# Two transformer blocks on one core: 96 tokens instead of 64 taken out of the dense expert products

## The chip, the cores and the metric

One Trainium2 chip, one core of it. The time is device microseconds of one launch. Single-core program, so there is one span and one granted TensorE clock.

## What is computed

512 tokens of width 1024 go through two blocks. The first ends in a layer of 16384 tiny experts, of which every token uses 128 (8 heads times 16); the second is attention with a gated feed-forward part and is not touched here. Cut to the expert layer:

```python
def block(xb):                                   # 128 tokens at a time
    q = (xb @ w_q).reshape(p, 8, 2, 64)
    sc = einsum('phcd,hcnd->phcn', q, sub_keys)  # 2 x 128 scores per head
    top_s, top_i = lax.top_k(sc, 16)
    cand_s = top_s[:, :, 0, :, None] + top_s[:, :, 1, None, :]
    best_s, best_pos = lax.top_k(cand_s, 16)     # 16 experts per head
    idx = take_along_axis(cand_i, best_pos)      # number = first * 128 + second
    g = softmax(best_s)
    act = gelu(einsum('phkd,pd->phk', expert_u[idx], xb))
    return einsum('phk,phkd->pd', g * act, expert_v[idx])
```

All in float32; the kernel splits each float32 operand into a high and a low float32r part and makes three products of them.

## The kernel before

**Dense and picked tokens.** The experts are 16 groups (`N_GROUPS`) of 8 tiles (`GROUP`) of 128. For the first `DT = T - PICKED` tokens (448) the kernel computes all 16384 experts densely: 128 U products `hidden = gelu(U h)`, a multiplication by a sparse table of coefficients (`weight`, "mix"), and 128 V products. Each product is one weight block of 128x1024 and 24 matmuls of 128x128 against `DT` columns (`partial`: 16 with the high weights, then 8 with the low ones). The last `PICKED` tokens (64) go another way: their 128 experts each are fetched as rows by number and used by VectorE alone. 64 tokens fill 128 partitions twice, so token t stands on two partitions with half of its experts each, and one indirect DMA fetches one row of 1024 per partition (512 KB).

**Row steps** (`row_step(q)` on VectorE, `load_rows(q)` on GpSimd). Steps 0 to `PICKED - 1` multiply a row of U by the token and sum (`row_coef`); then one gelu on ScalarE; steps `PICKED` to `2 * PICKED - 1` add coefficient times row of V to `own_sum`. The rows go round `ROWS` = 4 buffers; a load waits for the step that used its buffer before. At the end one matmul per output tile with `fold` adds the two partitions of each token. `ROW_STEPS` spreads the 128 steps evenly over the V slots of groups i = 1 to 14.

**Order of stages.** `w_in`, `w_out`, `w_q`; then the U stage: 120 U products (`AHEAD` = 15 groups), whose hidden tiles of 14 groups (`KEPT`) are put into DRAM. Beside it VectorE routes (`route_tokens`, four blocks of 128 tokens): for blocks 0 and 1 GpSimd scatters the 256 sets of coefficients into DRAM by accumulating indirect DMAs; for blocks 2 and 3 they are made by one-hot products, four tokens at a time ("quads": `make_hot`, four 256-wide matmuls at `place`, `placed_quad`). `QUADS_AT` says at which U product a quad is made: block 2 has 32 quads, block 3 has (448 - 384) / 4 = 16, one at every second product from number 83.
Then the loop over `MIX_ORDER` = 14, 15, 0, 1, ..., 13, whose index is i. At i = 0 the last 8 U products run, each beside one mix step of group 14; then each group has 8 V slots (k = 0 to 7). A slot has on VectorE: `split_lo` of the weight block of the next slot (`lo = raw - hi`), one `mix_tile` of the next group with its low part (`finish_mix`), at i = 0 an addition to the residual that waits for the slot's V product, then the row steps of that slot. ScalarE makes the high parts of the weights and of the mix. 17 steps of a rotation table (`table_steps`) stand one per slot in later groups.

**Queues.** SyncE loads weight blocks into `RAW` = 3 buffers, each when the low part three blocks before is made. GpSimd's in-order queue has, per group, its row loads, and after the fourth of them `load_group(i + 2)`: coefficient table and hidden tiles, 1792 KB each (128 x 8 x 448 x 4 bytes), which go through the same DMA queue as the rows. It waits first for the scatter to end and for the last stores of stage.

Of the kernel before, what the change touches and what calls it, by code (L numbers as in the profile page):

```python
# [37 lines left out]
PICKED = 64  # L38
DT = T - PICKED
ROWS = 4  # L40
SCATTERED = 2
ROUTE_STEPS = HEADS + HEADS // 2 + 4 + 2
# [141 lines left out]
def build(nc, a, out_cols, values, counting):  # L184

    with ExitStack() as ctx:
# [6 lines left out]
        def signal(name, step=1):  # L193
# [19 lines left out]
        scattered = [signal(f"scattered{tb}", 16) for tb in range(SCATTERED)]  # L213
        rows_landed = [signal(f"rows{i}_landed", 16) for i in range(ROWS)]
# [88 lines left out]
        own_x = sb("own_x", [P, D], F32, scope)  # L303
# [3 lines left out]
        fold = sb("fold", [P, PICKED], F32, scope)  # L307
        route = ExitStack()
        top_s = sb("top_s", [P, HEADS, 2, TOPK], F32, route)
# [30 lines left out]
        mixed = [(mixed_hi, mixed_lo), (h_hi, h_lo), (last_hi, last_lo)]  # L340
        position = sb("position", [P, T], I32, scope)
        turns = sb("turns", [P, T], F32, scope)
        own_sum = sb("own_sum", [P, D], F32, scope)
        rows = [sb(f"rows{i}", [P, D], F32, scope)[:] for i in range(2)] \
            + [t[:].rearrange("p k t -> p (k t)") for t in (square, scaled)]
# [124 lines left out]

        ROW_STEPS = {}
        for q in range(2 * PICKED):
            ROW_STEPS.setdefault(divmod(GROUP + q * (N_GROUPS - 2) * GROUP // (2 * PICKED), GROUP), []).append(q)

# [64 lines left out]
        def tensor():  # L539
# [280 lines left out]
            for i, g in enumerate(MIX_ORDER):  # L820
# [4 lines left out]
                for k in range(KD):  # L825
# [3 lines left out]
                    else:  # L829
# [277 lines left out]
        def scalar():  # L1107
# [523 lines left out]
        def vector():  # L1631
# [304 lines left out]
            def route_tokens(tb):  # L1936
# [84 lines left out]
            V.tensor_tensor(fold[:], const("ident")[:, 0:PICKED], const("ident")[:, PICKED:P], ALU.add).then_inc(*dve.inc("fold"))  # L2021
# [4 lines left out]
            ada_columns(40, 48, 0.0, "gate2")  # L2026
            for j in range(AHEAD * GROUP):
# [54 lines left out]
            def row_step(q):  # L2082

                kind, s = divmod(q, PICKED)
                row = rows[q % ROWS]
                if q == 0:
                    V.wait_ge(*act["own_x", 1])
# [4 lines left out]
                if kind == 0:  # L2092
                    V.tensor_tensor_reduce(out=row, in0=row, in1=own_x[:], scale=1.0, scalar=0.0, op0=ALU.mult, op1=ALU.add,  # L2093
                                           accum_out=row_coef[:, s:s + 1]).then_inc(*dve.inc(("row", q)))
                elif s == 0:
                    V.tensor_scalar(own_sum[:], row, row_coef[:, 0:1], None, ALU.mult).then_inc(*dve.inc(("row", q)))
# [750 lines left out]
```

## Time and profile before

| | |
|---|---|
| median of 3 runs | 2380.35 us (2378.09 to 2387.47) |
| profiled execution | 2381.73 us, span 2380.4 us |
| granted TensorE clock, mean | 0.987 |
| busy: PE, PEld | 2313.4, 2025.2 us |
| busy: DVE, ACT, POOL | 1578.9, 856.4, 951.0 us |
| U products 0 to 127 | 310 to 979 us |
| V products | 979 to 1603 us |

PE is TensorE's matmuls, PEld its weight loads, DVE VectorE, ACT ScalarE, POOL GpSimd, SP SyncE. A busy PE is not a PE at its peak; what tells its pace is the distance from the start of one matmul to the start of the next. "weights_lo" written by DVE is `split_lo`; "hidden<-hidden,weight" and "mixed_lo" or "h_lo" are the two parts of a mix step; "CUSTOM_DVE" on rows is a U row step; "own_sum<-rows,row_coef,own_sum" is a V row step. In a row, the bracket is the engine's idle time before the instruction and what ended it.

### The profile page before, as it was taken

The numbers are of one execution on the slowest core, as the hardware profiler recorded it, in microseconds if no ns is written. First come the engines' busy times: TensorE is split into PE (matmuls) and PEld (weight loads), VectorE is DVE, ScalarE is ACT, GpSimd is POOL, SyncE is SP. The second block draws the span as 40 slices with busy tenths as digits, with TensorE's granted clock in tenths as the row PEclk, the third lists the DMA queues.
The fourth block names the chain that finished last, engine by engine and source line by source line (L and its number), as shares of the span: only waits on it lengthen the run. The fifth ranks groups of instructions, "written<-read, shape, count | busy, mean of one in ns | idle before, by whom it ended". The sixth has DMA issues, their size and how long they took to land.

```text
span 2380.4 us, 29901 instructions
## 1 busy us (share of the span) xinstructions
PE 2313.4 (97%) x11272; PEld 2025.2 (85%) x11272; DVE 1578.9 (66%) x3014; ACT 856.4 (36%) x1335; POOL 951.0 (40%) x602
## 2 busy tenths in 40 slices
PE   6999999999899999999999999999999989999998
PEld 3777889999789999999999999998887778888887
DVE  6774699889996553588777777764856556434333
ACT  4433443333334333333333333353345534322221
POOL 1444208788888770033333433343332331111100
PEclk9999999999999999999999999999999999999999
DMA  7658746666667676579888888842424252333332
GB/s 289 195 148 251 211 138 170 162 153 160 163 150 188 169 182 206 196 301 343 322 321 330 315 349 298 300 132 86 130 67 116 70 188 89 97 97 98 102 98 76
DMA packets 199798, 443.60 MB, mean 186 GB/s; under 512 B 49180, under 2 KB 108700, under 8 KB 195104
## 3 DMA queue, kind: packets, MB, share of 16 engines
q1 hardware_dynamic: 139960, 319.12, 41.1%
q0 software_dynamic: 59696, 122.58, 17.3%
q8 instruction: 91, 1.49, 0.3%
q14 instruction: 51, 0.42, 0.1%
HBM read 374.06 MB, written 65.21 MB: 185 GB/s over the span
## 4 chain that ended last, share of the span: by engine, by line
PE 68%; DVE 3%; ACT 1%; issue 0%; ACTq 0%
PE bank L558 18%; PE bank L559 18%; PE bank L562 18%; PE bank_stat L935 1%; PE bank_stat L936 1%; PE bank_stat L940 1%; PE bank_stat L558 1%; PE bank_stat L562 1%; PE bank_stat L559 1%; DVE hot_weight L2010 1%; PE bank L967 1%; PE bank L965 1%; PE bank L980 1%; PE bank L710 1%; DVE weights_lo L1643 0%; PE bank_stat L585 0%
## 5 line engine op out<-in xcount | busy, mean ns | idle before, releaser
L558 PE MATMUL bank<-h_lo,weights_hi 128*128 128x448 f32 (+1 forms) x2148 | 813.8, 379 | 8.5 <-DVE gates L2311 3.8
L559 PE MATMUL bank<-h_hi,weights_hi 128*128 128x448 f32 (+1 forms) x2148 | 809.7, 377 | 0.0
L1119 ACT ACTIVATE weights_hi<-weights_raw 128x1024 fp32r<-128x1024 f32 (+1 forms) x411 | 432.1, 1052 | 498.1 <-PE bank L562 364.0
L1643 DVE TENSOR_TENSOR weights_lo<-weights_raw,weights_hi 128x1024 fp32r<-128x1024 f32 x351 | 443.6, 1264 | 196.9 <-ACT weights_hi L1119 194.5
L2489 POOL DMA_INDIRECT expert_coefs<-square x256 | 443.0, 1730 | 155.4 <-issue 79.0
L562 PE MATMUL bank<-h_hi,weights_lo 128*128 128x448 f32 (+1 forms) x2148 | 499.5, 374 | 1.4 <-DVE weights_lo L1643 1.4
L558 PEld LDWEIGHTS bank<-h_lo,weights_hi 128*128 128x128 f32 x2148 | 408.9, 190 | 61.3 <-DVE gates L2311 3.9
L559 PEld LDWEIGHTS bank<-h_hi,weights_hi 128*128 128x128 f32 x2148 | 408.5, 190 | 49.9 <-issue 0.2
L562 PEld LDWEIGHTS bank<-h_hi,weights_lo 128*128 128x128 f32 x2148 | 403.0, 188 | 52.3 <-DVE weights_lo L1643 2.5
L2436 POOL TENSOR_TENSOR weights_lo<-weights_raw,weights_hi 128x1024 fp32r<-128x1024 f32 x60 | 147.6, 2465 | 223.5 <-ACT weights_hi L1119 223.4
L1330 ACT ACTIVATE hidden<-bank 128x448 f32<-128x448 f32 x128 | 69.9, 546 | 406.4 <-PE bank L562 406.4
L558 PE MATMUL bank<-mixed_lo,weights_hi 128*128 128x448 f32 x456 | 166.5, 365 | 0.0
L559 PE MATMUL bank<-mixed_hi,weights_hi 128*128 128x448 f32 x456 | 166.5, 365 | 0.0
L2559 POOL TENSOR_TENSOR silu<-silu,ffn_scale 128x512 f32<-128x512 f32 x22 | 33.7, 1532 | 208.0 <-ACT silu L1614 208.0
L562 PE MATMUL bank<-mixed_hi,weights_lo 128*128 128x448 f32 x456 | 101.7, 365 | 0.0
L558 PEld LDWEIGHTS bank<-mixed_lo,weights_hi 128*128 128x128 f32 x456 | 85.7, 188 | 6.8
L562 PEld LDWEIGHTS bank<-mixed_hi,weights_lo 128*128 128x128 f32 x456 | 85.7, 188 | 6.8
L559 PEld LDWEIGHTS bank<-mixed_hi,weights_hi 128*128 128x128 f32 x456 | 85.6, 188 | 6.7
L2447 POOL TENSOR_TENSOR scaled<-scaled,square 128x512 f32<-128x512 f32 x18 | 25.5, 1416 | 150.5 <-ACT square L1266 148.9
L2061 DVE TENSOR_TENSOR hidden<-hidden,weight 128x448 f32<-128x448 f32 x128 | 79.1, 618 | 0.0
L2517 POOL DMA_INDIRECT rows<-in_rows_u,row_at x32 | 45.7, 1430 | 76.6 <-DVE row_coef L2093 73.9
L2548 POOL TENSOR_SCALAR scaled<-scaled,att_stats 128x384 f32<-128x384 f32 (+1 forms) x32 | 44.6, 1407 | 78.7 <-DVE att_stats L2288 78.7
(463 smaller groups left out, 3424.7 us busy)
## 6 DMA issues: line engine op xcount, KB each, us to landing
weights_raw<-in_expert_u SPq DMA_DIRECT2D x128, 512.0 KB, 3.8
weights_raw<-in_expert_v SPq DMA_DIRECT2D x128, 512.0 KB, 4.6
weight<-expert_coefs POOLq DMA_DIRECT2D x16, 1792.0 KB, 10.0
hidden_store<-hidden SPq DMA_DIRECT2D x28, 896.0 KB, 6.1
hidden<-hidden_store POOLq DMA_DIRECT2D x14, 1792.0 KB, 15.1
ada_raw<-in_w_ada SPq DMA_DIRECT2D x34, 512.0 KB, 6.1
expert_coefs<-zeros SPq DMA_DIRECT2D x32, 512.0 KB, 6.4
expert_coefs<-stage SPq DMA_DIRECT2D x12, 1024.0 KB, 5.8
```

The costliest lines, as they stand in the source:

```text
L558: M.matmul(bank[:, 0:width], hi[:, c:c + P], m_lo[k][:, 0:width], start=start and i == 0, stop=False)
L559: M.matmul(bank[:, 0:width], hi[:, c:c + P], m_hi[k][:, 0:width], start=False, stop=False)
L562: ins = M.matmul(bank[:, 0:width], lo[:, c:c + P], m_hi[k][:, 0:width], start=False, stop=stop and i == len(tiles) - 1)
L1119: S.activation(w_hi[n % SPLIT][:, 0:w], w_raw[n % RAW][:, 0:w], ACT.Copy).then_inc(*hi_done.inc(n))
L1330: S.activation(hidden[g % 2][:, n, :], banks["u", j][:, 0:DT], ACT.Gelu).then_inc(*act.inc(("u", j)))
L1643: V.tensor_tensor(w_lo[n % SPLIT][:, 0:w], w_raw[n % RAW][:, 0:w], w_hi[n % SPLIT][:, 0:w].bitcast(F32), ALU.subtract).then_inc(*lo_dve.in ...
L2061: V.tensor_tensor(v, v, weight[g % 2][:, :, n, :], ALU.mult).then_inc(*dve.inc(("mixed", g, n)))
L2436: G.tensor_tensor(w_lo[n % SPLIT][:, 0:w], w_raw[n % RAW][:, 0:w], w_hi[n % SPLIT][:, 0:w].bitcast(F32), ALU.subtract).then_inc(*lo_pool.i ...
L2489: G.indirect_dma_start(out=coef_store[:], out_offset=bass.IndirectOffsetOnAxis(ap=place_at[:, tb, c:c + 1], axis=0), in_=share[:, tb, c:c ...
L2517: G.indirect_dma_start(out=rows[q % ROWS], out_offset=None, in_=a[("rows_u", "rows_v")[kind]], in_offset=bass.IndirectOffsetOnAxis(ap=row_ ...
L2548: G.tensor_scalar(p, p, stats[:, u, 2:3], None, ALU.mult).then_inc(*pool.inc(("att_prob", u)))
L2559: G.tensor_tensor(silu[:, f % 2, :], silu[:, f % 2, :], ffn_scale[:], ALU.mult).then_inc(*pool.inc(("silu", f)))
```

## The change

`PICKED` becomes 96 and `DT` 416. The 96 tokens are taken in three batches of 32; in a batch each token stands on four partitions with a quarter of its experts. There are 192 row steps instead of 128, over 124 slots: the second four U slots of i = 0 and all V slots of i = 0 to 14 (before: 112 slots). `ROWS` is 5, the fifth buffer lying where the table's source and scratch lie, so its first load waits for the end of `table_steps`; those now run three per U slot at i = 0. The tokens are copied once onto their partitions by 12 DMAs (`copy_own`, on SyncE's queue after the last quad) in place of four ScalarE copies. `fold` adds four identity columns in three chained steps, and stands behind the first eight routing steps; the closing product is three 32-wide matmuls per tile instead of one of 64. Block 3 has (416 - 384) / 4 = 8 quads. The routing numbers of the picked tokens are made by two operations and 24 copies of 32x32 instead of six operations. `load_group` comes after the fifth row load of a group.

```diff
-PICKED = 64
+PICKED = 96
+BATCH = 32
+BATCHES = PICKED // BATCH
 DT = T - PICKED
-ROWS = 4
+ROWS = 5
...
+        SLOTS = [(0, "u", n) for n in range(HALF, GROUP)] + [(i, k) for i in range(N_GROUPS - 1) for k in range(KD)]
         ROW_STEPS = {}
         for q in range(2 * PICKED):
-            ROW_STEPS.setdefault(divmod(GROUP + q * (N_GROUPS - 2) * GROUP // (2 * PICKED), GROUP), []).append(q)
+            ROW_STEPS.setdefault(SLOTS[q * len(SLOTS) // (2 * PICKED)], []).append(q)
...
-            room = min(QUADS, AHEAD * GROUP - 2 - first)
+            room = min(n_quads * TB // 2, QUADS, AHEAD * GROUP - 2 - first)
...
-                            ins = M.matmul(held_bank(k)[:, DT:T], own_sum[:, k * P:(k + 1) * P], fold[:], start=True, stop=True)
+                            for b in range(BATCHES):
+                                ins = M.matmul(held_bank(k)[:, DT + b * BATCH:DT + (b + 1) * BATCH], own[b][:, k * P:(k + 1) * P],
+                                               fold[:], start=True, stop=True)
...
-                    for half in range(2):
-                        S.activation(own_x[half * PICKED:(half + 1) * PICKED, c * T:(c + 1) * T], banks["own_x", c][0:PICKED, :], ACT.Copy) \
-                            .then_inc(*act.inc(("own_x", c) if half else ("own_x_first", c)))
+                    S.activation(own_tokens_x[0:PICKED, c * T:(c + 1) * T], banks["own_x", c][0:PICKED, :], ACT.Copy) \
+                        .then_inc(*act.inc(("own_x", c)))
...
-                    for half, to in enumerate((slice(64, 128), slice(0, 64))):
-                        slots = slice(half * PICKED, (half + 1) * PICKED)
-                        V.tensor_copy(row_share[to, :], chosen[64:128, 2, slots]).then_inc(*dve.inc(("row_share", half)))
-                        chain(V.scalar_tensor_tensor(row_coef[to, :], chosen[64:128, 0, slots], float(N_KEYS), chosen[64:128, 1, slots],
-                                                     ALU.mult, ALU.add))
-                        chain(V.tensor_copy(row_at[to, :], row_coef[to, :]), ("row_at", half))
+                    chain(V.scalar_tensor_tensor(place_f, chosen[:, 0, :], float(N_KEYS), chosen[:, 1, :], ALU.mult, ALU.add))
+                    chain(V.tensor_copy(column_u, place_f), "row_numbers")
+                    for b in range(BATCHES):
+                        tokens = slice(P - PICKED + b * BATCH, P - PICKED + (b + 1) * BATCH)
+                        columns_of = slice(b * BATCH, (b + 1) * BATCH)
+                        for part in range(P // BATCH):
+                            to = slice(part * BATCH, (part + 1) * BATCH)
+                            V.tensor_copy(row_share[to, columns_of], chosen[tokens, 2, to]).then_inc(*dve.inc(("row_share", b, part)))
+                            V.tensor_copy(row_at[to, columns_of], column_u[tokens, to]).then_inc(*dve.inc(("row_at", b, part)))
...
                 if q == 0:
-                    V.wait_ge(*act["own_x", 1])
+                    V.wait_ge(*own_copied[BATCHES - 1, P // BATCH - 1])
...
                         split_lo(BLOCK_AT["expert_u", (g + 1) * GROUP + n] + 2)
+                        for _ in range(TABLE_STEPS // GROUP + 1):
+                            next(turning, None)
+                        for q in ROW_STEPS.get((i, "u", n), ()):
+                            row_step(q)
...
             load_group(0)
+            G.dma_start(position[:], a["positions"]).then_inc(*position_landed.inc("position"))
             load_group(1)
-            G.dma_start(position[:], a["positions"]).then_inc(*position_landed.inc("position"))
...
                 if q >= ROWS:
                     G.wait_ge(*dve["row", q - ROWS])
+                elif rows[q] is rows[-1]:
+                    G.wait_ge(*dve["angle"])
...
-            for half in range(2):
-                G.wait_ge(*dve["row_at", half])
-            load_group(2)
-            for i in range(1, len(MIX_ORDER)):
+            G.wait_ge(*dve["row_at", BATCHES - 1, P // BATCH - 1])
+            G.wait_ge(*own_copied[BATCHES - 1, P // BATCH - 1])
+            for n in range(GROUP):
+                for q in ROW_STEPS.get((0, "u", n), ()):
+                    load_rows(q)
+            for i in range(len(MIX_ORDER)):
...
+            def copy_own():
+
+                Y.wait_ge(*dve["routed", TB - 1])
+                Y.wait_ge(*act["own_x", 1])
+                for b in range(BATCHES):
+                    for part in range(P // BATCH):
+                        Y.dma_start(own[b][part * BATCH:(part + 1) * BATCH, :], own_tokens_x[b * BATCH:(b + 1) * BATCH, :]) \
+                            .then_inc(*own_copied.inc((b, part)))
```

## Rows read from the trace of the kernel before

**Rows 1.** The page: busy time, and VectorE's share in 40 slices.

```profile
PE 2313.4 (97%) x11272; PEld 2025.2 (85%) x11272; DVE 1578.9 (66%) x3014; ACT 856.4 (36%) x1335; POOL 951.0 (40%) x602
DVE  6774699889996553588777777764856556434333
```

**Rows 2.** Timeline (start, duration, engine, line): first matmul of two V blocks.

```profile
1105.43 0.36 PE L558 MATMUL bank<-h_lo,weights_hi 128*128 128x448 f32 x1
...
1144.34 0.36 PE L558 MATMUL bank<-mixed_lo,weights_hi 128*128 128x448 f32 x1
```

**Rows 3.** Timeline of PE: matmuls with 512 columns, then with 256.

```profile
2200.60 0.39 PE L558 MATMUL bank<-h_lo,weights_hi 128*128 128x512 f32 x1
...
2206.04 0.39 PE L558 MATMUL bank<-h_lo,weights_hi 128*128 128x512 f32 x1
...
2362.19 0.28 PE L710 MATMUL bank<-ffn_lo,weights_hi 128*128 128x256 f32 x1
...
2363.99 0.28 PE L710 MATMUL bank<-ffn_hi,weights_hi 128*128 128x256 f32 x1
```

**Rows 4.** Timeline of PE: two U blocks with a quad's products between.

```profile
750.80 1.78 PE L562 MATMUL bank<-h_hi,weights_lo 128*128 128x448 f32 x8
752.42 0.64 PE L805 MATMUL bank<-hot_weight,one_hot 128*128 128x256 f32 x4
756.14 1.78 PE L562 MATMUL bank<-h_hi,weights_lo 128*128 128x448 f32 x8
```

**Rows 5.** Windows: length, busy of PE, PEld, DVE, ACT, POOL, clock, DMA share, GB/s.

```profile
354.00:536.00 182.00, 182.00 (x902) 168.67 (x900) 158.75 (x508) 62.98 (x84) 145.53 (x86) 1.00 0.67 164
548.00:732.00 184.00, 168.31 (x842) 152.30 (x842) 182.09 (x543) 65.56 (x123) 156.86 (x90) 0.97 0.68 163
742.00:905.00 163.00, 163.00 (x832) 151.55 (x831) 92.89 (x209) 56.59 (x96) 121.74 (x71) 1.00 0.72 175
940.00:1570.00 630.00, 630.00 (x3112) 583.95 (x3111) 457.02 (x604) 206.01 (x272) 203.40 (x156) 1.00 0.79 296
```

**Rows 6.** Timeline of DVE in a V group: a row stall, then one slot.

```profile
1186.82 1.22 DVE L2093 CUSTOM_DVE_ANT_0 rows<-rows,own_x 128x1024 f32<-128x1024 f32 x1
...
1192.30 1.23 DVE L2093 CUSTOM_DVE_ANT_0 rows<-rows,own_x 128x1024 f32<-128x1024 f32 x1 [4.25 <-DMA rows<-in_rows_u,row_at]
...
1193.44 1.22 DVE L1643 TENSOR_TENSOR weights_lo<-weights_raw,weights_hi 128x1024 fp32r<-128x1024 f32 x1
...
1195.65 1.22 DVE L2093 CUSTOM_DVE_ANT_0 square<-square,own_x 128x1024 f32<-128x1024 f32 x1
...
1196.80 1.22 DVE L1643 TENSOR_TENSOR weights_lo<-weights_raw,weights_hi 128x1024 fp32r<-128x1024 f32 x1
```

**Rows 7.** The same view, later: two row steps of V in one slot.

```profile
1357.94 2.66 DVE L2099 SCALAR_TENSOR_TENSOR own_sum<-rows,row_coef,own_sum 128x1024 f32<-128x1024 f32 x2
```

**Rows 8.** Timeline of POOL: the group's hidden tiles, then the next row load.

```profile
1174.75 0.60 POOL L2506 DMA_DIRECT2D hidden<-hidden_store  x1
1175.66 1.41 POOL L2517 DMA_INDIRECT rows<-in_rows_u,row_at  x1 [0.30 <-issue]
```

**Rows 9.** Windows, columns as in rows 5: inside that burst, and a whole group.

```profile
1185.00:1190.00 5.00, 5.00 (x27) 4.63 (x26) 3.04 (x5) 1.56 (x3) 0.94 (x1) 1.00 0.99 415
...
1183.00:1222.00 39.00, 39.00 (x195) 36.14 (x194) 28.21 (x43) 12.34 (x16) 13.07 (x11) 1.00 0.85 323
```

**Rows 10.** Timeline of POOL: the last scatter, then the first tables.

```profile
895.13 1.54 POOL L2489 DMA_INDIRECT expert_coefs<-square  x1 [0.30 <-issue]
913.66 1.18 POOL L2502 DMA_DIRECT2D weight<-expert_coefs  x2 [16.99 <-DMA expert_coefs<-stage]
```

**Rows 11.** Timeline of DVE at i = 0: the residual waits for its product.

```profile
1013.21 0.68 DVE L2114 SCALAR_TENSOR_TENSOR residual<-bank,ada,residual 128x448 f32<-128x448 f32 x1 [1.98 <-PE bank L562]
```

**Rows 12.** Timeline of PE in the last group: two closing products.

```profile
1577.68 0.33 PE L837 MATMUL bank<-fold,own_sum 128*128 128x64 f32 x2
...
1582.77 0.33 PE L837 MATMUL bank<-fold,own_sum 128*128 128x64 f32 x2
```

More of the change, by code:

```diff
@@ L37 @@
 QUADS = P // 4
-PICKED = 64
+PICKED = 96
+BATCH = 32
+BATCHES = PICKED // BATCH
 DT = T - PICKED
-ROWS = 4
+ROWS = 5
 SCATTERED = 2
+TABLE_STEPS = 17
 ROUTE_STEPS = HEADS + HEADS // 2 + 4 + 2
@@ L213, in build @@
         scattered = [signal(f"scattered{tb}", 16) for tb in range(SCATTERED)]
+        own_copied = signal("own_copied", 16)
         rows_landed = [signal(f"rows{i}_landed", 16) for i in range(ROWS)]
@@ L302, in build @@
         hidden.append(sb("hidden1", [P, GROUP, DT], F32, scope))
-        own_x = sb("own_x", [P, D], F32, scope)
         row_at = sb("row_at", [P, PICKED], U32, scope)
@@ L306, in build @@
         row_coef = sb("row_coef", [P, PICKED], F32, scope)
-        fold = sb("fold", [P, PICKED], F32, scope)
+        fold = sb("fold", [P, BATCH], F32, scope)
+        sb("row_spacer", [P, 64], F32, scope)
         route = ExitStack()
+        sb("route_spacer", [P, 1408], F32, route)
         top_s = sb("top_s", [P, HEADS, 2, TOPK], F32, route)
@@ L340, in build @@
         mixed = [(mixed_hi, mixed_lo), (h_hi, h_lo), (last_hi, last_lo)]
+        over = ExitStack()
+        row_over = sb("row_over", [P, D], F32, over)
+        over.close()
         position = sb("position", [P, T], I32, scope)
         turns = sb("turns", [P, T], F32, scope)
-        own_sum = sb("own_sum", [P, D], F32, scope)
+        own = [sb(f"own{b}", [P, D], F32, scope) for b in range(BATCHES)]
         rows = [sb(f"rows{i}", [P, D], F32, scope)[:] for i in range(2)] \
-            + [t[:].rearrange("p k t -> p (k t)") for t in (square, scaled)]
+            + [t[:].rearrange("p k t -> p (k t)") for t in (square, scaled)] + [row_over[:]]
+        own_tokens_x = scaled[:].rearrange("p k t -> p (k t)")
         scope.close()
@@ L2019, in placed_quad @@
                     V.tensor_tensor(at, placed_part(tb, quad, half, 1), at, ALU.add).then_inc(*dve.inc(("place", tb, quad, half)))
-            V.tensor_tensor(fold[:], const("ident")[:, 0:PICKED], const("ident")[:, PICKED:P], ALU.add).then_inc(*dve.inc("fold"))
             routers = [route_tokens(tb) for tb in range(TB)]
@@ L2026, in vector @@
             ada_columns(40, 48, 0.0, "gate2")
+            chain(V.tensor_tensor(fold[:], const("ident")[:, 0:BATCH], const("ident")[:, BATCH:2 * BATCH], ALU.add))
+            chain(V.tensor_tensor(fold[:], fold[:], const("ident")[:, 2 * BATCH:3 * BATCH], ALU.add))
+            chain(V.tensor_tensor(fold[:], fold[:], const("ident")[:, 3 * BATCH:P], ALU.add), "fold")
             for j in range(AHEAD * GROUP):
@@ L2082, in row_step @@
             def row_step(q):
-                kind, s = divmod(q, PICKED)
+                kind, c = divmod(q, PICKED)
+                b, s = divmod(c, BATCH)
                 row = rows[q % ROWS]
                 if q == 0:
-                    V.wait_ge(*act["own_x", 1])
+                    V.wait_ge(*own_copied[BATCHES - 1, P // BATCH - 1])
                 if q == PICKED:
@@ L2092, in row_step @@
                 if kind == 0:
-                    V.tensor_tensor_reduce(out=row, in0=row, in1=own_x[:], scale=1.0, scalar=0.0, op0=ALU.mult, op1=ALU.add,
-                                           accum_out=row_coef[:, s:s + 1]).then_inc(*dve.inc(("row", q)))
+                    V.tensor_tensor_reduce(out=row, in0=row, in1=own[b][:], scale=1.0, scalar=0.0, op0=ALU.mult, op1=ALU.add,
+                                           accum_out=row_coef[:, c:c + 1]).then_inc(*dve.inc(("row", q)))
                 elif s == 0:
-                    V.tensor_scalar(own_sum[:], row, row_coef[:, 0:1], None, ALU.mult).then_inc(*dve.inc(("row", q)))
+                    V.tensor_scalar(own[b][:], row, row_coef[:, c:c + 1], None, ALU.mult).then_inc(*dve.inc(("row", q)))
                 else:
                     V.wait_ge(*dve["row", q - 1])
-                    V.scalar_tensor_tensor(own_sum[:], row, row_coef[:, s:s + 1], own_sum[:], ALU.mult, ALU.add) \
+                    V.scalar_tensor_tensor(own[b][:], row, row_coef[:, c:c + 1], own[b][:], ALU.mult, ALU.add) \
                         .then_inc(*dve.inc(("row", q)))
@@ L2120, in vector @@
                         dve.also(("held", k), ("x2", g, k))
-                    if i >= len(MIX_ORDER) - KEPT:
-                        next(turning, None)
                     for q in ROW_STEPS.get((i, k), ()):
@@ L2658, in sync @@
                     store_stage(*LAST_QUAD)
+                    copy_own()
                 load_weights(BLOCK_AT["expert_u", j] + 5)
```

4 lines of the change are left out of this document (2 added, 2 removed).

## The prediction

> **What bounds the kernel now.** I read the page first: PE is busy 97% and VectorE 66%, but VectorE's slices run from 3 to 9 tenths [rows 1], so the mean hides stages with different limits. Then the timeline of PE for its pace. In the V groups the first matmuls of two blocks eight apart are 38.91 us apart: 4.864 us per block of 24 matmuls, or 202.7 ns each [rows 2], and PE never stops from 940 to 1570 us [rows 5]. So there the pace of PE is the time. The windows over the U stage show three parts [rows 5]: U products 8 to 47 (354 to 536 us, PE full, VectorE 158.8 of 182 us), the 32 quads of block 2 (548 to 732 us, VectorE 182.1 of 184 us, PE only 168.3), and from 742 us on PE full again with VectorE little used. Only in the second is VectorE the bound; the first eight U products are another such place (VectorE at 9 tenths there [rows 1], my reading).
>
> **A dense block gets 32 columns shorter.** 448 columns take 202.7 ns [rows 2], 512 take (2206.04 - 2200.60) / 24 = 226.7 ns, 256 take 1.80 / 15 = 120 ns [rows 3]. From 256 to 512 that is 0.417 ns per column, so 32 columns are 13.3 ns and a block 24 x 13.3 = 0.32 us. 416 columns are not in the trace: 448 costs 2.7 ns more than the line of the other two widths (200.0). The line gives 186.7 ns for 416, the slope from 448 to 512 gives 190.7. I take 189.3, which keeps 448's excess, so 4.544 us per block; both ends stay in the range. The weight loads lie 120 ns apart where matmuls have 256 columns [rows 3], so they set no floor at 189.
> Beside it a rule. The Trainium skill (TensorE: Matmul & The Clock Gate, Back-to-back issue gap) gives sustained spacings of 81 ns for 128 columns and 131 ns for 512, 0.13 ns per column; by it a block would lose 24 x 4.2 = 0.10 us only. The trace's spacings are other ones, and its slope is three times that.
>
> **Where these 0.32 us count.** There are 256 such blocks. The first 8 are paced by VectorE, and so are the 32 of block 2's quads, whose VectorE work the change leaves alone: the stretch stays 184 us whatever PE could do [rows 5]. Elsewhere 256 - 40 = 216 blocks x 0.32 = **69.1 us**, if VectorE keeps up. For U products 8 to 47: 158.8 us of work in 182 x 4.544 / 4.864 = 170 us; it fits. From 742 us it fits easily, and block 3 makes 8 quads fewer. A block with a quad takes 756.14 - 750.80 = 5.34 us against 4.86 [rows 4], so 8 x 0.48 = **3.8 us** more.
>
> **Small things.** The closing product costs 5.09 - 4.86 = 0.22 us per tile [rows 12]; three of half the width I bound between twice and three times that plus nothing for the width, +0.14 to +0.45 us, and take 0.28: 8 tiles, **-2.2 us**. `fold` becomes three chained small operations in VectorE's first stretch: 0.3 us (0 to 0.6, an estimate: two operations more, far smaller than the 0.54 us that one of 448 columns takes [rows 6]). The 24 small copies come after product 80, where VectorE is idle half the time [rows 5], so nothing; without that cover some 3 us. `copy_own` puts 12 issues and 1.5 MB in front of a weight load on SyncE. In that stretch DMA is 72% busy [rows 5]; the transfer is 1.5 MB at 415 GB/s [rows 9], 3.7 us. Weight blocks are three ahead, so I take 1 us of 0 to 5. The four ScalarE copies that go save nothing, ScalarE is 36% busy [rows 1]. Sum so far: 69.1 + 3.8 - 2.2 - 0.3 - 1.0 = 69.4 us.
>
> **Scatter and tables.** GpSimd's scatter has its own pace and ends at 895 us; the first tables then waited 17 us for the last stores of `stage` [rows 10]. Those stores come 16 products earlier now. The U stage is some 30 us shorter (80 x 0.32 + 3.8), so the first mix of group 14, at about 937 us before, wants its table at 907; issued at about 900 us it lands by 911. VectorE waits some 4 us there; with 93 of 163 us busy in the stretch before [rows 5] it comes there far ahead of PE, so PE sees nothing. What is late next here is the scatter itself.
>
> **The V groups: is VectorE still covered?** One slot with one row step takes 1196.80 - 1193.44 = 3.36 us of VectorE: a low part 1.13, two mix parts 0.54 each, the row step 1.15 [rows 6]. Mixes get 0.03 us shorter each. A V row step costs about 1.19 alone, 1.28 when it follows another (2.66 for two, overlap taken in) [rows 7]. After the change a group has 192 x 8 / 124 = 12.4 row steps instead of 9.1: 8 x 2.13 + 12.4 x 1.15 = 31.3 us in the U half, 32.2 us in the V half. PE takes 8 x 4.544 = 36.35 us. So 5.0 and 4.1 us per group are left, where there were 38.9 - 28 = 11.
> Against this stands the stall behind the group's burst. GpSimd issues hidden tiles at 1174.75 and a row load right behind at 1175.66 [rows 8]; VectorE waits 4.25 us for that row until 1192.30 [rows 6], so the row needs 16.6 us. In the burst DMA is full at 415 GB/s [rows 9]. After the change the burst is 0.26 MB smaller (0.6 us), and four rows lie ready instead of three: 4 / 1.55 slots x 4.544 = 11.7 us of cover where there were 12.5. Stall: 16.6 - 0.6 - 11.7 = 4.3, or 6 us if VectorE runs at its own pace and eats the rows sooner. I take 4.6, near the stall seen. The group then needs 35.9 us in the U half (covered by 36.35) and 36.8 to 38.4 in the V half (not covered). The first group, i = 0, is the tightest: its residual additions hold VectorE to PE's pace with 2 us idle per slot [rows 11], and 1.5 row steps now go there, so VectorE enters group 1 with no lead. I cost it at 1.2 us there, 0.5 us in each of 7 groups of the U half and 0.7 us in each of 7 of the V half, rounded to **-10 us**; 0 to 20 by the ends of the stall.
> Is DMA itself full? Per group 8 weight blocks 4.2 MB, rows 6.5 MB, tables and hidden tiles 3.4 MB: 14.1 MB, 34.0 us at 415 GB/s, against 36.35. Before it was 12.65 MB in 38.9 us, 325 GB/s, which the window confirms (323, share 0.85) [rows 9]. So DMA goes from 85% to about 95% of what it can do. That is the thinnest cover of all.
>
> **Sum.** 69.4 - 10 = 59.4 us off the profiled execution of 2381.7: 2322.3. The median of the runs stands 1.4 us below that execution, so **2321 us**, 2.5% less.
>
> **Rivals.**
> (A) All cover holds and 416 columns fall on the line: nothing lost in the V groups (2311), and 216 x 24 x 2.7 ns = 14 us more from the width (2297). For it: a full lead of VectorE before the change. 22%.
> (B) Rows become the pace of the V groups. With a stall of 6.2 to 9 us a group takes 37.5 to 40.3 us in the U half and 38.4 to 41.2 in the V half; over 7 and 8 groups 25 to 66 us of the 69 are given back: 2335 to 2377, middle 2345. For it: DMA near full, one in-order queue for rows and tables. Against it: the burst gets smaller and the buffers more. 20%.
> (C) DMA from HBM is capped below what the burst shows. If a whole group could sustain only 358 GB/s, 14.1 MB take 39.4 us, 15 x 3.05 = 46 us lost: 2357. For it: no whole group has shown over 330. Against it: 415 GB/s over 5 us, more than once [rows 9]. 4%. The Trainium skill (DMA: Bandwidth & Descriptors, its table at the head) gives 358 GB/s as the limit of HBM per core. The trace exceeds it in the burst.
> (D) Slower than before. The same stall at 11 us: if each of 12.4 row loads per group waits for its full turn behind tables and weights, a group takes 42.3 and 43.2 us, 96 us lost, 27 more than all gains: about 2407. It decides at a group of 36.35 + 69.4 / 15 = 41.0 us, a stall of about 9. Seen so far: 4.25 in the rows above. 5%.
> (E) The change doesn't do what it says: the distance between matmuls stays near 203 ns at 416 columns. Then the gain is 3.8 us of quads less 3.5 of small things: 2380. 4%. By the skill's spacings above, 216 x 0.10 = 22 us would be gained.
> Forecast (2311 to 2335, likeliest 2321): 45%.
>
> **How the numbers follow.** The range takes in A nearly to its end and B past its middle: 2298 to 2357; outside are the last of A, B beyond 2357, half of C, D and E, together some 19%. A measurement of this kernel tells about 0.5% (12 us) from no change. Faster by more than that, under 2368: forecast, A, C and nearly all of B, 0.89. Within: E and the end of B, 0.06. Slower: D, 0.05.
>
> **What would show it.** Right: V blocks 4.54 us apart nearly everywhere; the window of block 2's quads still 184 us with VectorE at 99%; U stage ending near 900 us; one row stall of 4 to 6 us per group, DMA share near 0.95. Wrong: PE waiting for weights_lo in most groups (B), DMA full through whole groups (C), matmuls 203 ns apart (E), or PE waiting for mixed at i = 0, which would make the scatter the late one.

## The result and the profile after

The changed kernel takes 2364.91 us (median of 5 runs, 2362.95 to 2367.24), the kernel before 2380.35 (5 runs, 2378.09 to 2387.47): ratio 0.9931, interval 0.9914 to 0.9948. So 15 us were gained by the medians, 17 by the profiled executions, of the 59 predicted, and the time lies above the upper end of the range. The profiled execution is 2364.91 us, its span 2363.6.

Where the time went is read from four marks: the gelu of U product 0, the gelu of U product 120, the last closing product, the end of the span. The column "predicted" is the prediction's sum split over the same stretches.

| stretch, us | before | predicted | after |
|---|---|---|---|
| to U product 0 | 310.0 | 310.3 | 311.0 |
| U product 0 to 120 | 635.1 | 606.7 | 603.4 |
| U product 120 to last closing product | 658.1 | 626.8 | 673.2 |
| from there to the end | 777.2 | 777.2 | 776.0 |
| span | 2380.4 | 2321.0 | 2363.6 |

The U stage came out as forecast, 3 us better. The V stage got 15 us longer where it was to get 31 us shorter. All of the miss is there: 46.4 us, of which the other stretches give 3.8 back.

The page of after, its busy times and the chain that ended last (answers to [rows 1]):

```profile
PE 2249.3 (95%) x11272; PEld 2031.7 (86%) x11272; DVE 1616.6 (68%) x3044; ACT 850.0 (36%) x1317; POOL 1062.2 (45%) x666
...
PE 34%; DMA 11%; DVE 11%; POOL 3%; issue 2%; ACT 1%; DVEq 0%; ACTq 0%
```

PE was 68% of that chain before and VectorE 3%; now DMA and VectorE have 11% each, most of it in lines named after rows. PE's busy time fell by 64 us, the span by 17: the rest is idle time of PE. The pace of PE where nothing holds it, from the timeline of PE (start, duration, engine, line), two pairs of U blocks and then a pair of closing products, the answer to [rows 2, 12]:

```profile
503.48 0.35 PE L568 MATMUL bank<-h_lo,weights_hi 128*128 128x416 f32 x1
...
506.50 1.67 PE L572 MATMUL bank<-h_hi,weights_lo 128*128 128x416 f32 x8
508.00 0.35 PE L568 MATMUL bank<-h_lo,weights_hi 128*128 128x416 f32 x1
...
862.21 1.66 PE L572 MATMUL bank<-h_hi,weights_lo 128*128 128x416 f32 x8
...
866.69 1.66 PE L572 MATMUL bank<-h_hi,weights_lo 128*128 128x416 f32 x8
...
1571.51 0.75 PE L848 MATMUL bank<-fold,own 128*128 128x32 f32 x6
...
1576.72 0.75 PE L848 MATMUL bank<-fold,own 128*128 128x32 f32 x6
```

A block takes 508.00 - 503.48 = 4.52 us early in the U stage and 866.69 - 862.21 = 4.48 us later (there from one block's low products to the next one's): 188.3 and 186.7 ns per matmul of 416 columns. The closing product lies 5.21 us apart, 0.69 to 0.73 more than a block without it.

The windows (length, busy of PE, PEld, DVE, ACT, POOL, clock, DMA share, GB/s) over U products 8 to 47, over block 2's quads, over the rest of the U stage, and over the whole V stage, the answers to [rows 5]:

```profile
354.00:536.00 182.00, 182.00 (x971) 180.89 (x970) 171.68 (x553) 67.43 (x92) 140.78 (x83) 1.00 0.70 171
545.00:730.00 185.00, 164.05 (x851) 158.17 (x850) 180.66 (x543) 65.12 (x123) 157.56 (x91) 0.94 0.67 161
742.00:905.00 163.00, 163.00 (x884) 162.57 (x883) 66.32 (x115) 56.03 (x86) 129.41 (x78) 1.00 0.74 182
926.00:1588.00 662.00, 624.59 (x3221) 607.90 (x3220) 531.29 (x704) 220.92 (x288) 330.18 (x228) 0.97 0.88 329
```

In the last one PE stands 37 us, and it starts matmuls below its pace beside that: the granted clock is 0.97 there, where it was 1.00 [rows 5]. Before the change PE was full from 940 to 1570.

**One V group, as they all go.** POOL's timeline, the group's burst and the row loads around it (answer to [rows 8]); then VectorE's (answer to [rows 6]); then PE's:

```profile
1156.25 0.58 POOL L2521 DMA_DIRECT2D weight<-expert_coefs  x1
1156.80 0.61 POOL L2525 DMA_DIRECT2D hidden<-hidden_store  x1
1157.71 1.38 POOL L2538 DMA_INDIRECT row_over<-in_rows_u,row_at  x1 [0.30 <-issue]
...
1176.68 1.68 POOL L2538 DMA_INDIRECT row_over<-in_rows_u,row_at  x1 [7.90 <-DVE row_coef L2110]
```

```profile
1166.36 1.22 DVE L2110 CUSTOM_DVE_ANT_0 scaled<-scaled,own 128x1024 f32<-128x1024 f32 x1
1167.50 0.08 DVE L2110 DVE_READ_ACCUMULATOR2_ANT row_coef<- 128x1 f32 x1
1175.18 1.23 DVE L2110 CUSTOM_DVE_ANT_0 row_over<-row_over,own 128x1024 f32<-128x1024 f32 x1 [7.60 <-DMA row_over<-in_rows_u,row_at]
1176.33 0.08 DVE L2110 DVE_READ_ACCUMULATOR2_ANT row_coef<- 128x1 f32 x1
1176.33 1.22 DVE L1654 TENSOR_TENSOR weights_lo<-weights_raw,weights_hi 128x1024 fp32r<-128x1024 f32 x1
```

```profile
1177.60 3.14 PE L572 MATMUL bank<-h_hi,weights_lo 128*128 128x416 f32 x8 [2.94 <-DVE weights_lo L1654]
1180.55 0.55 PE L568 MATMUL bank<-h_lo,weights_hi 128*128 128x416 f32 x1
```

The row asked for at 1157.71, right behind 3.4 MB of tables and hidden tiles, is used at 1175.18: it is 17.5 us on its way (the "way"). The rows that lie ready last VectorE until 1167.58, 9.9 us (the "cover"). The difference, 7.6 us, VectorE stands; the low part of the next weight block is queued behind the row step, starts at 1176.33, and PE, which has gone on meanwhile, starts its low products only at 1177.60, when that part is done.

The stop has a second price on PE. These eight products take 2.95 us to the next start where the eight at 506.50 above take 1.50: the window around them shows a mean granted clock of 0.75, so part of it passed at the lower of the two levels (1.2 GHz in place of 2.4).

```profile
1175.00:1180.00 5.00, 2.40 (x7) 2.30 (x8) 4.82 (x8) 1.50 (x2) 1.71 (x2) 0.75 1.01 389
```

By the mean of 0.97 some 40 us of the V stage passed at that level (an estimate: 0.03 x 2 x 662). It does not set the time of a group: VectorE, at whose pace the groups go, waits in them for nothing that PE makes.

This happens once per group, 14 times from 977 us on: the row is 17.2 to 19.4 us on its way (mean 17.8), the ready rows cover 9.9 to 12.3 us (mean 10.5), the stall is 6.1 to 9.1 us (mean 7.3). VectorE's waits for rows in the V stage, by tile:

```profile
DVE row_over L2110 <- DMA row_over<-in_rows_u,row_at: 28.4, 4, 7.6
DVE own L2116 <- DMA scaled<-in_rows_v,row_at: 26.5, 4, 6.9
DVE rows L2110 <- DMA rows<-in_rows_u,row_at: 22.6, 3, 8.2
DVE own L2116 <- DMA rows<-in_rows_v,row_at: 17.5, 3, 9.1
DVE own L2113 <- DMA rows<-in_rows_v,row_at: 7.4, 1, 7.4
DVE square L2110 <- DMA square<-in_rows_u,row_at: 6.5, 2, 6.1
```

With 0.2 us more that is 109.1 us; before, the same sum was 44.3. What VectorE waited for otherwise has gone: before, 44.8 us for `weights_hi` and 40.2 for `mixed_hi`, which ScalarE makes at PE's pace; after, none. So VectorE has no lead left to pay a stall from, and a group takes VectorE's own work plus the stall: from one stall's end to the next, 38.3 to 42.1 us, 39.85 on average (13 groups from 977.44 to 1495.47), where PE alone would need 36.

### The profile page after: what moved, and what is told of

Its sections match the earlier page's. It is cut to its first block, busy times and chain, and to the rows that moved or that the text cites. A ratio compares the mean times of both kernels' runs of the same rounds, so it can differ in the third digit from the quotient of the medians.

```text
span 2363.6 us, 29994 instructions
## 1 busy us (share of the span) xinstructions
PE 2249.3 (95%) x11272; PEld 2031.7 (86%) x11272; DVE 1616.6 (68%) x3044; ACT 850.0 (36%) x1317; POOL 1062.2 (45%) x666
## 4 chain that ended last, share of the span: by engine, by line
PE 34%; DMA 11%; DVE 11%; POOL 3%; issue 2%; ACT 1%; DVEq 0%; ACTq 0%
PE bank L568 8%; PE bank L572 8%; PE bank L569 8%; DMA row_over<-in_rows_u,row_at 2%; DMA rows<-in_rows_v,row_at 2%; DVE own L2116 2%; DMA scaled<-in_rows_v,row_at 2%; DVE weights_lo L1654 2%; DMA square<-in_rows_u,row_at 2%; DMA rows<-in_rows_u,row_at 2%; DVE hidden L2077 1%; PE bank_stat L947 1%; PE bank_stat L948 1%; PE bank_stat L952 1%; DVE rows L2110 1%
## 5 line engine op out<-in xcount | busy, mean ns | idle before, releaser
L568 PE MATMUL bank<-h_lo,weights_hi 128*128 128x416 f32 (+1 forms) x2148 | 796.0, 371 | 10.2 <-DVE gates L2330 3.8
L569 PE MATMUL bank<-h_hi,weights_hi 128*128 128x416 f32 (+1 forms) x2148 | 791.1, 368 | 0.0
L572 PE MATMUL bank<-h_hi,weights_lo 128*128 128x416 f32 (+1 forms) x2148 | 482.8, 366 | 15.8 <-DVE weights_lo L1654 15.4
L1342 ACT ACTIVATE hidden<-bank 128x416 f32<-128x416 f32 x128 | 66.2, 518 | 347.2 <-PE bank L572 331.6
L568 PE MATMUL bank<-mixed_lo,weights_hi 128*128 128x416 f32 x456 | 163.5, 358 | 6.6 <-ACT mixed_hi L1406 6.2
L569 PE MATMUL bank<-mixed_hi,weights_hi 128*128 128x416 f32 x456 | 161.6, 354 | 0.0
L572 PE MATMUL bank<-mixed_hi,weights_lo 128*128 128x416 f32 x456 | 102.2, 369 | 17.9 <-DVE weights_lo L1654 17.9
L2538 POOL DMA_INDIRECT rows<-in_rows_v,row_at x39 | 62.4, 1599 | 61.1 <-DVE own L2116 45.4
L2538 POOL DMA_INDIRECT rows<-in_rows_u,row_at x39 | 56.7, 1454 | 59.3 <-DVE row_coef L2110 53.5
L2077 DVE TENSOR_TENSOR hidden<-hidden,weight 128x416 f32<-128x416 f32 x128 | 74.7, 583 | 10.0 <-DMA weight<-expert_coefs 9.9
```

Of the source, the lines that this page charges most:

```text
L568: M.matmul(bank[:, 0:width], hi[:, c:c + P], m_lo[k][:, 0:width], start=start and i == 0, stop=False)
L569: M.matmul(bank[:, 0:width], hi[:, c:c + P], m_hi[k][:, 0:width], start=False, stop=False)
L572: ins = M.matmul(bank[:, 0:width], lo[:, c:c + P], m_hi[k][:, 0:width], start=False, stop=stop and i == len(tiles) - 1)
L1342: S.activation(hidden[g % 2][:, n, :], banks["u", j][:, 0:DT], ACT.Gelu).then_inc(*act.inc(("u", j)))
L2077: V.tensor_tensor(v, v, weight[g % 2][:, :, n, :], ALU.mult).then_inc(*dve.inc(("mixed", g, n)))
L2538: G.indirect_dma_start(out=rows[q % ROWS], out_offset=None, in_=a[("rows_u", "rows_v")[kind]], in_offset=bass.IndirectOffsetOnAxis(ap=row_ ...
```

## Experiments

Three theories could make the V stage long. **T1**: the row loads stand in one in-order queue behind the burst; neither VectorE nor DMA is full by itself. **T2**: VectorE has no room for 12.4 row steps per group. **T3**: DMA has no room for the bytes of a group. The kernels before in these runs had medians of 2380.86 to 2383.23, so ratios are given. "V stage" is the stretch from U product 120 to the last closing product, 673.2 us in the changed kernel.

**1. The burst in eight pieces (spread8).** Four over the token sets of the table, four over pairs of hidden tiles, one behind each row load from the second on.

```diff
-            def load_group(i):
+            def group_parts(i):
...
-                    G.dma_start(weight[g % 2][:].rearrange("p s j t -> p (s j t)"),
-                                coefs[g].rearrange("p s j t -> p (s j t)")).then_inc(*weight_landed[g % 2].inc(g))
+                    for c in range(4):
+                        s = slice(c * n_s // 4, (c + 1) * n_s // 4)
+                        G.dma_start(weight[g % 2][:, s].rearrange("p s j t -> p (s j t)"),
+                                    coefs[g][:, s].rearrange("p s j t -> p (s j t)")).then_inc(*weight_landed[g % 2].inc((g, c)))
...
+                        yield
...
-                    if n == ROWS - 1:
-                        load_group(i + 2)
+                    if n >= 1:
+                        next(parts, None)
```

> The changed kernel with each group's table and hidden tiles (3.4 MB) fetched in 8 pieces, one behind each of 8 row loads, instead of two transfers behind the fifth row load. Theory 1 (the row load queued behind that burst stalls VectorE some 7 us per group, and VectorE has only 4 to 5 us to spare): the stall falls under 2 us, V groups come to 36.2 to 36.6 us instead of 37.8 to 43.3, and the whole takes 2310 to 2325 us. Theory 2 (VectorE's row steps are simply too much work) and theory 3 (DMA is full over whole groups): within 5 us of the changed kernel, 2360 to 2370.

Measured: 2331.03 us (2328.03 to 2333.69), ratio 0.9777 (0.9761 to 0.9794), V stage 635.8. The same bytes, the same row steps, 34 us less than the changed kernel: only their order in the queue is another. VectorE's row waits fall from 109.1 to 66.6 us, in 58 small ones of at most 5.3. The time is 6 us above the range that T1 expected. POOL's timeline shows what it still pays:

```profile
994.00 0.57 POOL L2525 DMA_DIRECT2D weight<-expert_coefs  x1 [6.19 <-DVE h_lo L1696]
994.88 1.35 POOL L2554 DMA_INDIRECT rows<-in_rows_u,row_at  x1 [0.30 <-issue]
```

The first piece now comes so early that its buffer is still in use by the mix of the group before; POOL waits 6.19 us for that mix, with all row loads behind it.

**2. What is each resource worth alone?** no_rows leaves out the row loads and the row steps, loads_only the steps alone (each load waits for the landing of the one that used its buffer), steps_only all row loads but the first five (the steps then work on stale rows, and those of U with a factor of 0.02 in place of 1). All three leave out or falsify the part of the output that belongs to the 96 picked tokens.

```diff
 def row_step(q):
+                if q == PICKED - 1:
+                    V.memset(row_coef[:], 0.0).then_inc(*dve.inc(("row", q)))
...
+                return
```

```diff
 def load_rows(q):
                 if q >= ROWS:
-                    G.wait_ge(*dve["row", q - ROWS])
+                    return
```

> The changed kernel without row loads and without row steps (the picked tokens' expert part is left out). All theories: V groups at PE's pace, 36.2 us, about 2305 us; it gives the floor of the narrower products. If it stays above 2340, the loss is in none of the rows' parts.

> The changed kernel with all 192 row loads but without VectorE's row steps (left out); a load waits for the landing five before in place of the step. Theory 1 and 2: V groups at 36.2 us, about 2307 us, DMA share about 0.95. Theory 3: groups stay at 38 us or more, 2340 or more, with DMA share near 1.0 throughout.

> The changed kernel with all 192 row steps on VectorE but only the first five row loads (the others are left out; the steps work on what lies in the buffers). Theory 1 and 3: V groups at 36.2 to 36.5 us, about 2310 us, PE never waiting for weights_lo. Theory 2: groups stay at 38 us or more, 2345 or more.

| | us | ratio (interval) | V stage |
|---|---|---|---|
| no_rows | 2302.28 | 0.9661 (0.9641 to 0.9680) | 608.9 |
| loads_only | 2307.92 | 0.9684 (0.9665 to 0.9704) | 614.1 |
| steps_only | 2308.79 | 0.9688 (0.9663 to 0.9713) | 621.1 |
| changed kernel | 2364.91 | 0.9931 (0.9914 to 0.9948) | 673.2 |

The windows 1100 to 1500 of the changed kernel, loads_only and steps_only, in this order:

```profile
1100.00:1500.00 400.00, 377.07 (x1930) 366.58 (x1929) 321.27 (x413) 126.69 (x163) 208.68 (x145) 0.97 0.94 355
```

```profile
1100.00:1500.00 400.00, 400.00 (x2132) 397.59 (x2130) 195.98 (x263) 136.19 (x182) 147.21 (x146) 1.00 0.92 364
```

```profile
1100.00:1500.00 400.00, 400.00 (x2128) 397.61 (x2127) 349.78 (x435) 135.74 (x181) 9.42 (x18) 1.00 0.56 198
```

All loads without the steps: PE is full, and DMA moves 364 GB/s, more than in the changed kernel, at a lower busy share. All steps without the loads: VectorE does 349.78 us of work in 400 and PE is full. Each costs 5 to 12 us of V stage by itself, the two together 64. In steps_only a part of the 12 is the wait for the fifth row at the start, which it keeps (VectorE 5.91 us, PE 3.31; experiment 4). T2 and T3 fall, each as the sole cause; what costs is the coupling, a step that waits for a load that waits in a queue.

**3. One buffer less (four_buffers).** If the stall is way minus cover, a fifth of the cover must come out as stall.

```diff
-ROWS = 5
+ROWS = 4
...
-            + [t[:].rearrange("p k t -> p (k t)") for t in (square, scaled)] + [row_over[:]]
+            + [t[:].rearrange("p k t -> p (k t)") for t in (square, scaled)]
...
-                elif rows[q] is rows[-1]:
-                    G.wait_ge(*dve["angle"])
```

> The changed kernel with four row buffers as before the change (and so without the fifth's wait for the table). If the cover of the stall is the rows that lie ready, one row less is 1/1.55 of a slot, some 2.9 us more stall behind each of 14 bursts: +40 us, less some 6 us for the wait at the start, about 2399 us (2388 to 2408), slower than before the change. If instead the moved bytes alone set the pace, within 5 us of the changed kernel (2365).

Measured: 2388.73 us (2382.02 to 2392.00, 6 runs), ratio 1.0025 (1.0008 to 1.0042), V stage 695.5: with four buffers the 96 tokens would have been no gain at all. One of its stalls, VectorE and the load that it waits for:

```profile
1053.48 1.23 DVE L2110 CUSTOM_DVE_ANT_0 scaled<-scaled,own 128x1024 f32<-128x1024 f32 x1 [9.99 <-DMA scaled<-in_rows_u,row_at]
```

```profile
1034.50 0.60 POOL L2525 DMA_DIRECT2D hidden<-hidden_store  x1
1035.40 1.39 POOL L2536 DMA_INDIRECT scaled<-in_rows_u,row_at  x1 [0.30 <-issue]
```

18.1 us on its way, as with five buffers, but covered by 8.1 us only. The direction held, the size not quite: 24 us in place of 34. Over the 14 long stalls the cover is 8.5 us where it was 10.5, a fifth less at VectorE's own pace (the 2.9 us expected were reckoned at PE's), but the way is shorter too, 17.3 in place of 17.8; the stall is 8.8 us in place of 7.3. VectorE's row waits rise from 109.1 to 132.8 us, some 1.6 us per group, and these 24 us are all that the kernel loses.

**4. Where the fifth buffer and the early start come in (fifth_later, rows_from_v).** In the changed kernel the fifth load of all waits for the end of the rotation table, and every load behind it too:

```profile
943.16 0.93 POOL L2538 DMA_INDIRECT row_over<-in_rows_u,row_at  x1 [33.13 <-DVE rotation_table L2096]
```

```profile
948.75 1.23 DVE L2110 CUSTOM_DVE_ANT_0 row_over<-row_over,own 128x1024 f32<-128x1024 f32 x1 [5.86 <-DMA row_over<-in_rows_u,row_at]
```

```profile
951.14 0.68 PE L568 MATMUL bank<-mixed_lo,weights_hi 128*128 128x416 f32 x1 [4.40 <-ACT mixed_hi L1406]
```

VectorE stands 5.86 us and PE 4.40. The first experiment uses the fifth buffer for the first time with load 8; the second gives the steps back to the V slots alone.

```diff
+        BUFFER = [q % 4 if q < 8 else (q - 4) % ROWS for q in range(2 * PICKED)]
...
-                row = rows[q % ROWS]
+                row = rows[BUFFER[q]]
```

```diff
-        SLOTS = [(0, "u", n) for n in range(HALF, GROUP)] + [(i, k) for i in range(N_GROUPS - 1) for k in range(KD)]
+        SLOTS = [(i, k) for i in range(N_GROUPS - 1) for k in range(KD)]
```

> The changed kernel with the fifth buffer first used by load 8 instead of load 4, so that no row load waits for the end of the table steps. Theory: the single stall at the start (5.9 us on VectorE, one block of 11.4 us on PE) goes, all other groups stay: 2357 to 2361 us. Rival (that block is late for another reason, the tables of group 14 or the residual additions): 2364 to 2366.

> The changed kernel with row steps only in the V slots of i = 0 to 14 (120 slots, 12.8 steps per group), none in the last U group. Theory: the early slots help little, because what limits is the stall per group: the block of 11.4 us goes (-7), VectorE has 0.4 us more per group (+6), 2360 to 2368 us. If VectorE's amount of work were the limit, every group would be longer by more than that and the time over 2372.

Measured: fifth_later 2363.74 us, 0.9926 (0.9906 to 0.9946); rows_from_v 2361.12 us, 0.9915 (0.9895 to 0.9935). Neither differs from the changed kernel by more than their intervals; but with two runs each these reach 5 us to either side, as far as the gain that was looked for. fifth_later does remove the stall of 5.86. In its profile the first burst still goes out at the same time as in the changed kernel, as POOL's timeline shows:

```profile
957.97 0.61 POOL L2526 DMA_DIRECT2D hidden<-hidden_store  x1
958.88 1.43 POOL L2540 DMA_INDIRECT scaled<-in_rows_u,row_at  x1 [0.30 <-issue]
```

The changed kernel issues the same load at 959.04; VectorE goes on with it at 977.08 in fifth_later and at 977.44 in the changed kernel. That is no proof that the gain is waited for again, because this execution came later to the V stage: its scatter, which the edit does not touch, ended 7.3 us later, and the first table went out so much later, at 903.24 in the changed kernel (first row) and at 910.59 in fifth_later (second).

```profile
903.24 0.61 POOL L2521 DMA_DIRECT2D weight<-expert_coefs  x1 [2.00 <-issue]
910.59 0.61 POOL L2522 DMA_DIRECT2D weight<-expert_coefs  x1 [2.04 <-issue]
```

The V stage of fifth_later is 666.6 us and that of rows_from_v 668.0, against 673.2. So the profiles speak for a price of 5 to 7 us of this wait, and the times cannot tell it from nothing; it stays open.

**5. The pieces later (spread_late), and both repairs (both).** The pieces stand behind the fifth row load and the ones after it, so that their buffers are free (`if n >= 4` in the loop above). The second kernel adds the `BUFFER` list of fifth_later.

> As spread8 (tables and hidden tiles in 8 pieces between row loads), but the first piece behind the fifth row load of the group, not the second, so that row loads are not held up by the wait for the group before (6 us per group in spread8). Theory 1: 2316 to 2326 us. If spread8's rest over its floor (2331 against 2308) is DMA being full (share 0.98), no change: 2329 to 2333.

> spread_late and fifth_later together. If the two losses are separate they add: 6 to 8 us under spread_late, about 2313 us (2308 to 2320).

Measured: spread_late 2315.20 us (2310.29 to 2317.13), ratio 0.9725 (0.9708 to 0.9741), V stage 616.0, 16 us under spread8, which a DMA without room would not have allowed; both 2308.12 us (2304.72 to 2309.42, 5 runs), ratio 0.9680 (0.9667 to 0.9693), V stage 614.4. The latter is faster than either kernel of this case: 57 us under the changed one, and its V stage is within 6 us of no row work at all. Its window and, from its page, the chain that ended last:

```profile
1100.00:1500.00 400.00, 400.00 (x2130) 397.61 (x2129) 350.00 (x435) 136.17 (x180) 248.18 (x206) 1.00 0.96 372
```

```profile
PE 68%; DVE 3%; DMA 0%; ACT 0%; issue 0%; ACTq 0%
```

VectorE has the same 350.00 us of work in 400 us as in steps_only, at full DMA traffic, 372 GB/s, and the chain is PE's again. Its row waits are 22.0 us, the longest 2.0; one of them, with the load that it waits for:

```profile
1014.46 1.23 DVE L2111 CUSTOM_DVE_ANT_0 rows<-rows,own 128x1024 f32<-128x1024 f32 x1 [1.95 <-DMA rows<-in_rows_u,row_at]
```

```profile
1001.20 0.59 POOL L2535 DMA_DIRECT2D hidden<-hidden_store  x1
1002.09 1.38 POOL L2556 DMA_INDIRECT rows<-in_rows_u,row_at  x1 [0.30 <-issue]
```

12.4 us on its way in place of 17.8, and 10.4 of cover: the cover is the same, the way is shorter. By the times the late fifth buffer is worth 0.45% here (the intervals 0.9708 to 0.9741 and 0.9667 to 0.9693 lie apart). The V stages of the two profiles differ by 1.6 us only, so where that gain comes from is not shown.

**6. The same pieces in the kernel before (before_spread).** The same edit on the kernel before, pieces behind its fourth row load.

> The kernel before the change (64 tokens, four buffers) with its tables and hidden tiles in 8 pieces, the first behind the fourth row load. Theory 1: PE was the bound there and the stalls were hidden, so no change: within 3 us of the kernel before. Rival (splitting the transfers is a gain by itself, in DMA or GpSimd): 10 us or more faster.

Measured: 2382.34 against 2383.23 us, ratio 0.9999 (0.9989 to 1.0009). The kernel before had such stalls in most groups too, 44.3 us in all, and PE saw none of them; with the pieces VectorE waits for no row at all, and the V stage is 658.1 us as before. So splitting the transfers is no gain by itself, and where VectorE has a lead, shortening its stalls is worth nothing.

## Why the prediction was wrong

**What failed** is one term of the sum, the 10 us for rows in the V groups. In its place stand some 52 us: a group took 39.85 us on average against the 36.35 that PE was to need, times 15. (Against no_rows, where PE runs a little faster than predicted, the V stage is 64.3 us longer.) The spread kernels show that most of it is the stall behind the burst. The mechanism was in the prediction (rival B, "rows become the pace of the V groups", 2335 to 2377, middle 2345), with the right rows behind it; it was given 20% and should have been the forecast. The measured time lies inside B's range. Its "middle 2345" is not the middle of 2335 and 2377, which is 2356; the forecast's range ended at 2357 and so left the upper half of B outside. Its price was taken from two numbers, and both missed to the same side:

- The way of the row. I took 16.6 us from one row and subtracted 0.6 for the smaller burst. Over the twelve groups of the kernel before in which VectorE waited it was 17.0 on average, and after the change it is 17.8. The burst is smaller, but more row loads go through the same queue, and DMA is full all the while, as the window over the flight of the row shown above tells (that these loads make up the difference is my reading, not shown):

```profile
1157.70:1175.20 17.50, 16.97 (x91) 16.59 (x90) 9.90 (x18) 4.72 (x6) 7.01 (x5) 1.00 0.99 399
```

- The cover. I took 11.7 us: four rows at PE's pace, 4 / 1.55 slots of 4.544. But in a group in which VectorE sets the pace it eats the rows at its own: 9.9 to 11.0 us of cover in all groups but the first. The prediction named that case ("or 6 us if VectorE runs at its own pace") and then chose "near the stall seen". That is circular: whether VectorE runs at PE's pace is just what the stall decides. The row that it was leaned on, 4.25 us [rows 6], was one of fourteen of 0.5 to 6.3 us, taken where VectorE still had a lead.

With 17.8 - 10.5 = 7.3 us and VectorE's own work (a group less its stall: mostly 31.2 us with 12 row steps of U and 32.5 with 12 of V, 32.3 to 33.8 with 13; predicted 31.3 and 32.2 for 12.4) a group takes 38.6 to 39.5 us by the prediction's own sum against 36.35, 15 groups some 40 us more; the rest up to the 39.85 measured is mostly VectorE's work, some 0.6 us per group above the prediction's. So the work of VectorE was right to two per cent; the idle time put beside it was not. The margin was 4 to 5 us per group, and the stall above it went to the end; in four_buffers 23.7 us more of row waits made the V stage 22.3 longer.

**A wait that was not priced.** The fifth buffer's first load waits for the end of `table_steps`, and it stands in the same in-order queue as all later loads. It took 5.86 us of VectorE and 4.40 of PE at i = 0; I had 1.2 us there. What it is worth is open: 5 to 7 us by the V stages of experiment 4 and nothing measurable by its times; 7 to 11 us by the times of experiment 5 and 1.6 by its V stages.

**The other steps.**
- Width of the dense blocks: right. 188.3 and 186.7 ns against 189.3; the lower one is the line through 256 and 512 columns to the tenth, so the 2.7 ns that 448 columns have above that line do not carry over. Why a kernel runs at 4.52 in one stretch and 4.48 in another stays open. Rival E is refuted. By the Trainium skill (TensorE: Matmul & The Clock Gate, Back-to-back issue gap) a block would have lost 0.10 us (an estimate); it lost 0.34 to 0.38.
- Block 2's quads: right. From product 48 to 80 193.3 us against 194.2 before, with VectorE at 180.66 of 185. The 0.32 us do not count there.
- Closing products: too cheap. Three of 32 columns cost 0.69 to 0.73 us per tile; with 0.22 before [rows 12] that is 0.47 to 0.51 more, where I took 0.28 and bounded at 0.45. Over 8 tiles 3.8 to 4.1 us, not 2.2. Per product that is 0.23 to 0.24 us at 32 columns and 0.22 at 64 [rows 12]: here they cost by their number, not by their columns.
- Scatter and tables: right in kind, 9.9 us for 4. The first mix stood at 933.2 us before, not at 937, so it came for its table some 4 us earlier than reckoned. It waited, and PE did not:

```profile
912.32 0.59 DVE L2077 TENSOR_TENSOR hidden<-hidden,weight 128x416 f32<-128x416 f32 x1 [9.86 <-DMA weight<-expert_coefs]
```

- DMA (rival C): refuted. loads_only moved 364 GB/s over 400 us in which PE never stopped, spread8 377 at a share of 0.98:

```profile
1100.00:1500.00 400.00, 392.22 (x2061) 383.25 (x2060) 348.36 (x437) 136.90 (x174) 240.08 (x214) 1.00 0.98 377
```

  The 358 GB/s of the Trainium skill (DMA: Bandwidth & Descriptors, its table at the head), there half of what a stack of HBM gives two cores, did not bind here, where one core runs.
- Slower than before (rival D): not with five buffers, but four_buffers is at that point, at long stalls of 7.2 to 10.0 us and 0.25% above the kernel before. The tipping point was computed as a stall of 9.

What stays open: how DMA shares its time between the queue of rows and tables and the queue of weights, and so why the way takes 17.2 us in one group and 19.4 in another. Part of the gain of the spread kernels may come from a smoother stream of weight blocks (ScalarE waited 146.3 us for them in the changed kernel from 1060 to 1560); no run separates that from the rows. In the changed kernel it did not reach VectorE, which never waited for the high part of a weight block in the V stage.

## What to carry to other kernels

A stall is the way of a transfer through everything queued ahead of it, less the time in which its consumer uses up what lies ready; work out the second at the consumer's own pace, not at that of the engine that it is about to hold up. When a small load that somebody waits for shares an in-order queue with a large one that nobody needs soon, cut the large one into pieces and put them between; here that was 34 to 50 us of 2365. A stall of an engine with a lead costs nothing, and the same stall costs in full once a change has eaten the lead, so price stalls against the margin that is left after the change.

## What the hardware showed unexpectedly

- A single core moved 377 GB/s over 400 us (DMA busy 0.98) and 385 over a group of the kernel with both repairs:

```profile
1150.00:1189.70 39.70, 39.70 (x213) 39.47 (x212) 34.72 (x55) 13.65 (x18) 24.71 (x22) 1.00 0.99 385
```

- The distance of matmuls is not linear in their columns at 448: 186.7 ns at 416 lies on the line through 120 (256) and 226.7 (512), 202.7 at 448 is 2.7 above it, and at 416 it can also stay at 188.3, as it does over U products 12 to 44 of the changed kernel (4.52 us each).
- Row loads with pieces of 0.43 MB between them are 11 to 14 us on their way where VectorE waits more than 1 us for them (both repairs), against 17 to 19 behind one burst of 3.4 MB. In the 17.5 us of the window above 399 GB/s are 7.0 MB: twice the burst, so by my reading the way of a row is mostly the bytes that DMA has to move ahead of it and beside it.
